# Modulation vectors as VectorE dot products along rows of turned weights, in a two-block transformer kernel on one core

## What is computed

```python
cond = silu(c)                                       # 1024 numbers
mod = (cond @ ada_w[l] + ada_b[l]).reshape(9, 1024)  # first block, nine vectors a layer
u = rmsnorm(h, gain) * (1.0 + mod[1]) + mod[0]
h = h + 0.5 * (1.0 + mod[2]) * swiglu(u, wg, wu, wd)
...
mod = silu(c_2) @ ada_w_2[l] + ada_b_2[l]            # second block, six vectors a layer
```

## Time and profile before

| | |
|---|---|
| runs | 2355.34, 2343.04, 2352.70 us; median 2352.7 |
| the profiled execution's own time | 2357.99 us |
| its span in the trace | 2356.2 us |
| mean granted TensorE clock | 0.961 of full speed |
| TensorE matmul busy | 2169.0 us (92%), 16352 matmuls |
| VectorE busy | 1649.2 us (70%) |
| ScalarE busy | 1055.9 us (45%) |
| GpSimd busy | 672.3 us (29%) |
| DMA | 465.39 MB, mean 198 GB/s |

### The profile page before, as it was taken

One profiled execution on the slowest core, in us unless ns is written; L12 is line 12 of the kernel. 1 busy time (PEld: TensorE's weight loads), 2 busy tenths in 40 slices (PEclk: granted clock), 3 DMA queues, 4 the chain that ended last, 5 costly groups with the idle time before them and its releaser, 6 DMA issues. The chain is left out here.

```text
span 2356.2 us, 38578 instructions
## 1 busy us (share of the span) xinstructions
PE 2169.0 (92%) x16352; PEld 2067.1 (88%) x16352; DVE 1649.2 (70%) x1821; ACT 1055.9 (45%) x1565; POOL 672.3 (29%) x294
## 2 busy tenths in 40 slices
PE   2999999989999998999899988999999888999998
PEld 2999898889999998888899976778999877879998
DVE  4777777787777777868767777865767867645555
ACT  2544566344445445563444354343444433435443
POOL 1233212212111121354233332423233424212222
PEclk9999999999999999999899988999999988998999
DMA  7677656457767776554477744545677643424553
GB/s 283 210 260 254 207 197 197 155 181 255 258 234 247 255 254 198 189 166 160 162 276 260 254 134 135 182 141 188 211 259 238 200 147 112 126 99 152 183 177 106
DMA packets 289789, 465.39 MB, mean 198 GB/s; under 512 B 11344, under 2 KB 231120, under 8 KB 289104
## 3 DMA queue, kind: packets, MB, share of 16 engines
q1 hardware_dynamic: 252320, 324.96, 42.4%
q10 hardware_dynamic: 37296, 137.97, 16.2%
HBM read 461.84 MB, written 1.05 MB: 196 GB/s over the span
## 5 line engine op out<-in xcount | busy, mean ns | idle before, releaser
L614 PE MATMUL bank<-u_high,high 128*128 128x256 f32 (+1 forms) x3248 | 943.1, 290 | 60.8 <-DVE u_low L1528 51.1
L614 PE MATMUL bank<-u_high,low 128*128 128x256 f32 (+1 forms) x3248 | 930.6, 287 | 0.0
L614 PE MATMUL bank<-u_low,high 128*128 128x256 f32 (+1 forms) x3248 | 930.5, 286 | 0.0
L1485 DVE TENSOR_TENSOR low<-ring,high 128x1024 fp32r<-128x1024 f32 x416 | 712.0, 1730 | 222.7 <-ACT high L1096 196.6
L1962 POOL TENSOR_TENSOR low<-ring,high 128x1024 fp32r<-128x1024 f32 x186 | 481.3, 2589 | 1258.4 <-ACT high L1096 1091.2
L614 PEld LDWEIGHTS bank<-u_high,high 128*128 128x128 f32 (+1 forms) x3248 | 628.8, 194 | 77.4 <-issue 48.4
L1096 ACT ACTIVATE high<-ring 128x1024 fp32r<-128x1024 f32 x602 | 601.1, 1042 | 160.7 <-PE bank L614 97.1
L614 PEld LDWEIGHTS bank<-u_low,high 128*128 128x128 f32 (+1 forms) x3248 | 624.8, 192 | 3.6 <-issue 2.7
L614 PEld LDWEIGHTS bank<-u_high,low 128*128 128x128 f32 (+1 forms) x3248 | 622.8, 192 | 0.4
L614 PE MATMUL bank<-xa,high 128*128 128x256 f32 x2368 | 433.7, 285 | 6.2 <-DVE low L1485 4.2
L614 PEld LDWEIGHTS bank<-xa,high 128*128 128x128 f32 x2368 | 370.6, 192 | 10.1 <-issue 4.9
(11 more groups left out here) (176 smaller groups left out, 2149.7 us busy)
## 6 DMA issues: line engine op xcount, KB each, us to landing
ada_ring<-ada ACTq DMA_DIRECT2D x256, 512.0 KB, 4.7
ring<-w_in SPq DMA_DIRECT2D x76, 1024.0 KB, 5.6
ring<-ffn_wg SPq DMA_DIRECT2D x44, 1024.0 KB, 6.4
ring<-ffn_wu SPq DMA_DIRECT2D x44, 1024.0 KB, 7.6
ring<-ffn_wd SPq DMA_DIRECT2D x44, 1024.0 KB, 5.9
ring<-ffn_w_gate_up SPq DMA_DIRECT2D x44, 1024.0 KB, 6.4
ring<-ffn_w_down SPq DMA_DIRECT2D x22, 1024.0 KB, 5.0
ring<-w_out SPq DMA_DIRECT2D x20, 1024.0 KB, 4.9
```

The source lines that it names most:

```text
L614: return pe.e.matmul(out, lhs, rhs, start=start, stop=stop, skip_group_check=True)
L1485: dve.e.tensor_tensor(lo, src, hi.bitcast(F32), ALU.subtract).then_inc(*dve.done(("low", n)))
```

## The change

A piece is now a slab of the turned weight: its 128 partitions are outputs, its free dimension the 1024 inputs. The host turns the weights (`layout`). Per piece VectorE makes one `scalar_tensor_tensor` that multiplies the slab with `cond`, which now lies in SBUF as a row of 1024 numbers per block copied to all 128 partitions, and sums along the row with `accum_out` into one column of `sums`. After a job's eight pieces VectorE adds the bias and writes `mods` in the same turn. ScalarE's `ada_high`, GpSimd's `ada_low`, the 16 matmuls of each job, their bank, and the tiles `ada_acc`, `ada_high`, `ada_low`, `ones_r` are gone. The loads of the pieces have the same sizes, queue, ring and waits as before. The two rows of `cond` (512 KB each) are two new loads on SyncE's queue, the first ahead of the parameters, the second behind the third fill; ScalarE applies Silu to 128 x 1024 for each, the second time between the issue of the constants and the first norm.

```diff
     def step(self):
-        total, self.split = self.split, self.full
-        split, self.full = self.full, None
...
-        return total, split, loads, piece
+        return loads, piece
...
     def until(self, job):
-        while JOB[job] not in self.summed:
+        while self.piece < KT * (JOB[job] + 1):
             yield self.step()
...
-        self.ada_acc = [self.sb(f"ada_acc{i}", D) for i in range(2)]
-        self.ada_low = [self.sb(f"ada_low{i}", D, F32R, at + 4 * D * i) for i in range(2)]
-        self.ada_high = self.sb("ada_high", D, F32R)
...
-        self.cond = self.sb("cond", 2 * KT)
+        self.cond = self.sb("cond", 2 * D)
+        self.sums = self.sb("sums", KT * len(JOBS))
...
-    def ada(turns):
-        for total, _, _, _ in turns:
-            if total is None:
-                continue
-            b = banks.take("work", "ada", total)
-            pe.wait_ge(("ada_low", total))
-            for j in range(KT):
-                mm(b[:, 2 * j:2 * j + 2], m.ada_high[:, j * P:(j + 1) * P], m.ones_r[:, 0:2], j == 0, False)
-                t = mm(b[:, 2 * j:2 * j + 2], m.ada_low[total % 2][:, j * P:(j + 1) * P], m.ones_r[:, 0:2], False, True)
-            t.then_inc(*pe.done(("ada_sum", total)))
...
     def ada(turns):
-        for _, split, loads, _ in turns:
-            if split is not None:
-                act.wait_ge(("ada", KT * split + KT - 1))
-                if split:
-                    act.wait_ge(("ada_sum", split - 1))
-                act.e.activation(m.ada_high[:, :], m.ada_acc[split % 2][:, :], ACT.Copy) \
-                    .then_inc(*act.done(("ada_high", split)))
+        for loads, _ in turns:
             for n in loads:
...
-    act.wait_ge(("params",), ("eps",), ("ones",))
-    act.e.activation(m.ones_r[:, :], m.ones[:, 0:2], ACT.Copy).then_inc(*act.done(("ones_r",)))
-    act.e.activation(m.cond[:, :], m.pc("c1", 0, 2 * KT), ACT.Silu).then_inc(*act.done(("cond",)))
+    act.wait_ge(("c", 0), ("eps",), ("ones",))
+    act.e.activation(m.cond[:, 0:D], m.cond[:, 0:D], ACT.Silu).then_inc(*act.done(("cond", 0)))
     ada(act.ada.until(("a", 1)))
...
     act.e.dma_start(m.cst[:, P:C1_W], dram["const1"][:, P:C1_W]).then_inc(*act.done(("c1",), sem="const", n=16))
+    act.wait_ge(("c", 1))
+    act.e.activation(m.cond[:, D:2 * D], m.cond[:, D:2 * D], ACT.Silu).then_inc(*act.done(("cond", 1)))
     for s in STAGES:
...
     def ada(turns):
-        for total, _, _, piece in turns:
...
-                dve.wait_ge(("cond",), ("ada_in", piece))
-                if k == 0:
-                    if job >= 2:
-                        dve.wait_ge(("ada_sum", job - 2))
-                    dve.e.tensor_scalar(to, w, m.cond[:, c:c + 1], None, ALU.mult).then_inc(*dve.done(("ada", piece)))
-                else:
-                    dve.wait_ge(("ada", piece - 1))
-                    dve.e.scalar_tensor_tensor(out=to, in0=w, scalar=m.cond[:, c:c + 1], in1=to, op0=ALU.mult,
-                                               op1=ALU.add).then_inc(*dve.done(("ada", piece)))
+        for _, piece in turns:
+            if piece is None:
+                continue
+            job, j = divmod(piece, KT)
+            block = "ab".index(JOBS[job][0])
+            w = m.ada_ring[:, piece % ADA_SLOTS * D:(piece % ADA_SLOTS + 1) * D]
+            dve.wait_ge(("cond", block), ("ada_in", piece))
+            dve.e.scalar_tensor_tensor(out=w, in0=w, scalar=1.0, in1=m.cond[:, block * D:(block + 1) * D],
+                                       op0=ALU.mult, op1=ALU.mult, accum_out=m.sums[:, piece:piece + 1]) \
+                .then_inc(*dve.done(("ada", piece)))
+            if j == KT - 1:
+                of = slice(KT * job, KT * (job + 1))
+                dve.wait_ge(("params",), ("ada", piece))
+                dve.e.tensor_tensor(m.mods[:, of], m.sums[:, of], m.pc("bias", KT * job, KT), ALU.add) \
+                    .then_inc(*dve.done(("mod", job)))
...
 def sp_program(sp, m, dram):
+    sp.e.dma_start(m.cond[:, 0:D], dram["cond"][:, 0:D]).then_inc(*sp.done(("c", 0), sem="c", n=16))
     sp.e.dma_start(m.par[:, :], dram["params"]).then_inc(*sp.done(("params",), sem="params", n=16))
...
         sp.e.dma_start(m.slot(n), f.source(dram)).then_inc(*sp.done(("fill", n), sem=f"fill{n % SLOTS}", n=16))
+        if n == 2:
+            sp.e.dma_start(m.cond[:, D:2 * D], dram["cond"][:, D:2 * D]).then_inc(*sp.done(("c", 1), sem="c", n=16))
...
-    ada1 = np.concatenate([i["ada_w"].reshape(LAYERS, D, 9, D).transpose(0, 2, 1, 3).reshape(LAYERS * 9, D, D),
+    ada1 = np.concatenate([i["ada_w"].reshape(LAYERS, D, 9, D).transpose(0, 2, 3, 1).reshape(LAYERS * 9, D, D),
...
+    cond = np.ascontiguousarray(np.broadcast_to(np.concatenate([i["c"][0], i["c_2"][0]])[None, :], (P, 2 * D)))
```

More of the change, by code:

```diff
@@ L59 @@
 PB_W = columns(PB, [("nm", 8), ("nf", 8), ("qn", 2), ("kvn", 1), ("gq", 1), ("gk", 1)])
-PC_W = columns(PC, [("c1", 8), ("c2", 8), ("fin", 8), ("out", 8), ("bias", 8 * len(JOBS))])
+PC_W = columns(PC, [("fin", 8), ("out", 8), ("bias", 8 * len(JOBS))])
 BASE_C = LAYERS * (PA_W + PB_W)
@@ L364, in __init__ @@
         self.piece = self.issued = 0
-        self.full = self.split = None
-        self.summed = set()
         self.due = 0.0
     def step(self):
-        total, self.split = self.split, self.full
-        split, self.full = self.full, None
-        if total is not None:
-            self.summed.add(total)
         loads = range(self.issued, min(self.piece + ADA_SLOTS, KT * len(JOBS)))
@@ L380, in step @@
             self.piece += 1
-            if piece % KT == KT - 1:
-                self.full = piece // KT
-        return total, split, loads, piece
+        return loads, piece
     def turns(self, rate):
@@ L706, in into_acc @@
             t.then_inc(*pe.done(("read", n)))
-            ada(pe.ada.turns(rate_of(keys[k])))
     def norm(s):
[L710 to L713, removed]
         b = banks.take("work", "norm", s)
@@ L996, in pe_program @@
         t.then_inc(*pe.done(("x_full", d // 2)))
-    pe.wait_ge(("ones_r",))
     for s in STAGES:
@@ L1005, in pe_program @@
             mixer2(s)
-        if s[0] not in ("fin", "out"):
-            ada(pe.ada.until(gate_of(s)[0]))
     for a in range(TT):
@@ L1941, in pool_program @@
 def pool_program(pool, m):
[L1942 to L1949, removed]
     def split(upto):
@@ L1968, in grains @@
             split(ahead_of(key))
-            ada(pool.ada.turns(rate_of(key)))
     def look_ahead(key):
@@ L1975, in norm @@
     def norm(s):
[L1976 to L1979, removed]
         look_ahead(first_grain(s))
@@ L2316, in parameters @@
         put(base, PB, "gk", column(np.tile(np.asarray(i["gqa_k_norm_g_2"][l]), 2), 1))
-    put(BASE_C, PC, "c1", column(i["c"][0], 8))
-    put(BASE_C, PC, "c2", column(i["c_2"][0], 8))
     put(BASE_C, PC, "fin", column(i["final_norm"], 8))
@@ L2345, in layout @@
     i = {k: np.asarray(v) for k, v in inputs.items()}
-    ada1 = np.concatenate([i["ada_w"].reshape(LAYERS, D, 9, D).transpose(0, 2, 1, 3).reshape(LAYERS * 9, D, D),
-                           i["final_ada_w"].reshape(D, 2, D).transpose(1, 0, 2)])
-    ada2 = np.ascontiguousarray(i["ada_w_2"].reshape(LAYERS, D, 6, D).transpose(0, 2, 1, 3)
+    ada1 = np.concatenate([i["ada_w"].reshape(LAYERS, D, 9, D).transpose(0, 2, 3, 1).reshape(LAYERS * 9, D, D),
+                           i["final_ada_w"].reshape(D, 2, D).transpose(1, 2, 0)])
+    ada2 = np.ascontiguousarray(i["ada_w_2"].reshape(LAYERS, D, 6, D).transpose(0, 2, 3, 1)
                                 .reshape(LAYERS * 6, D, D))
+    cond = np.ascontiguousarray(np.broadcast_to(np.concatenate([i["c"][0], i["c_2"][0]])[None, :], (P, 2 * D)))
     const1, const2 = constants()
     arrays = {n: np.ascontiguousarray(i[n]) for n in WEIGHTS}
-    arrays.update(x=np.ascontiguousarray(i["x"][0]), ada1=ada1, ada2=ada2, const1=const1, const2=const2,
+    arrays.update(x=np.ascontiguousarray(i["x"][0]), ada1=ada1, ada2=ada2, cond=cond, const1=const1, const2=const2,
                   params=parameters(i), na_bias=window_bias(i["na_rpb_2"]))
```

12 lines of the change are left out of this document (1 added, 11 removed).

## The result

The changed kernel takes 2288.9 us (median of 4 runs, 2286.1 to 2292.4) against 2352.9 for the kernel before, a ratio of 0.9744 with a 95% interval of 0.972 to 0.9767. The direction was right, the size was not. The profiled execution took 2291.4 us, 66.6 less than that of before. The changed kernel ran only with the result, so differences to it are good to some 3 us.

The account below looks back on a forecast made before the run. TensorE was taken to bound FFN stages, chains over other engines partly the mixers. Terms -33 - 7 - 4.5 + 2 + 5 = -37.5 us took the 2352.7 us median to 2315, range 2295 to 2339.

Parts of the forecast that it names:

- TensorE's matmuls: Removing each job's 16 matmuls saves 33 us in FFN stages, 7 in m1 and 4.5 in m2.
- GpSimd's subtractions: Removing GpSimd's 89.8 us over 30 jobs: an indirect gain through quicker VectorE, given no time in the sum.
- VectorE's pieces: Pieces with a row sum take 0.1 to 0.2 us more, hidden in FFN stages; net 2 us lost.
- the start: First fill 4 us earlier, but ScalarE waits for cond's second row before the first norm; 5 us lost.
- What bounds the kernel: FFN stages are TensorE's, by comparison with the last stage without jobs; mixers belong partly to chains over other engines.
- rival B: cond's second row lands early (9 us); mixers and slow FFN stage gain from GpSimd's relief (8 to 11); 2297; chance 0.20.
- FFN term: FFN stages: 19 jobs at 1.73 us of matmuls, all on the path, 33 us saved.
- The mixers' share: Matmuls removed in mixers: 70% of 10.4 us in m1 (7 us), half of 8.7 in m2 (4.5 us).
- ScalarE and GpSimd "counted at nothing": Neither engine is a bound; removing 31.4 us of ScalarE and 89.8 us of GpSimd gets no term in the sum.
- D: Row sum costs a second pass, 1.1 us more per piece; 76 us more, 2429 us; decisive from 0.6 us; chance 0.08.
- C: Only FFN stages gain; dearer pieces eat the mixers' share and the start loses 8 us; 2336 us; chance 0.12.
- E: Removal is worth nothing, TensorE's time for these matmuls being slack other engines fill; about 2350 us; chance 0.05.

Follow-up runs that it names:

- b_match: Kernel before with 64 bytes free before h and 32 before region, putting u and xa at the changed kernel's offsets within 128 bytes; 2334.9 us.
- a_mm: Changed kernel with 16 two-column matmuls per job put back on a tile of constants, without waits, result unread; 2315.4 us.
- a_pool: Changed kernel with one GpSimd subtraction of 128 x 768 on constants put back per job, 30 in all, result unused; 2303.7 us.
- a_back: Changed kernel with matmuls, GpSimd subtractions and the piece's scalar from SBUF put back together, without waits for other engines; 2328.9 us.
- a_twice: Changed kernel with each VectorE piece preceded by a second scalar_tensor_tensor on the same slab, without the sum, result unread; 2462.1 us.
- a_late: Changed kernel with cond's second row loaded behind fill 20 instead of 2, its Silu moved ahead of the first m1 stage's norm; 2277.9 us.
- b_up64: Kernel before with 64 bytes left free in front of h, putting u at 32 and xa at 64 within 128 bytes; 2330.0 us.
- a_up96: Changed kernel with 96 bytes left free in front of h, putting u at 0 and xa at 64 within 128 bytes; 2284.8 us.
- a_rel: As a_best, with the weight tiles high and low also moved by 64 bytes, so weights and moving operands all start at 64; 2284.6 us.
- a_best: Changed kernel with a_late's edit plus 32 bytes free before h and 64 before region, putting u and xa at 64; 2270.3 us.
- a_ptr: Changed kernel with the piece's constant scalar 1.0 read from a column of ones in SBUF; 2285.8 us, measured once.

## Why the prediction was wrong in size

| term | forecast, us | measured, us | by |
|---|---|---|---|
| places of `u` and `xa` | not in the sum | -15 | b_match |
| TensorE's matmuls | -44.5 | -26.5 | a_mm |
| GpSimd's subtractions | 0 | -15 | a_pool |
| VectorE's pieces, ScalarE, waits (6 to 8 us of it may be places) | +2 | -11 | left over, a_back |
| the start | +5 | +5 | first reciprocal |
| sum | -37.5 | -62.5 | -64 in all |

Without the 15 us of places the time would have been about 2304 us, inside the range; so the term that put the result below it is the one that the sum didn't have. That the rest comes near, -37.5 against -46, is in good part luck: the matmuls were put 18 us too high, GpSimd's subtractions 15 and the third group 13 too low.

**What bounds the kernel.** TensorE in the FFN stages was right, and reading it from the stage without jobs was the best step: its comparison gave 1.5 us per job for one stage and 2.9 for another, and a_mm gave 1.5. But the same comparison had 11.7 us for four jobs in the slow stage of the earlier trace rows, of which the matmuls are 6 to 7. I left the rest to rival B and held against it that the split of grains is unchanged; a_pool, in which that stage is 2.7 us longer than in the changed kernel, shows that GpSimd's subtractions are a part of it.

**TensorE's matmuls.** The mechanism held and the FFN term was near (28 for 33). The mixers' share was over-estimated: 11.5 us in the sum, about nothing in a_mm's total, with 5 us in the two m1 and no loss that shows in the two m2. There the failed step is taking a fixed share of TensorE's time in m2, where the trace shows chains over VectorE and ScalarE.

**ScalarE and GpSimd "counted at nothing".** Beside the places, this is the step of the argument that failed. Neither engine is a bound, and GpSimd idled 71% of the time, but of its 94 us of `ada_low` 76 overlapped VectorE's instructions on 128 x 1024, which take 1.3 us alone and up to 3.5 with it. I quoted the Trainium skill (SBUF — State Buffer, Who interferes with whom) for just this contention and then gave it a price only in rival B, together with an early landing that didn't come. The measured price is 15 us for 30 subtractions, 0.5 us each; the trace agrees with the rule.

**VectorE's pieces.** I expected 0.1 to 0.2 us more by ScalarE's accumulator row; the piece is 0.06 us shorter and its accumulator read adds 0.08 that overlaps the next instruction. Pieces in a row start 1.15 us apart, not 1.35. That FFN stages hide it was wrong for a dearer piece: a_twice shows 0.6 us lost per piece there at 1.2 us more, in stages where the changed kernel's VectorE is 77% busy. Idle time of an in-order engine that feeds the bound one is not slack to that amount. If the same holds in the other direction, a cheaper piece and quicker splits are worth something in FFN stages too.

**The start.** Right in mechanism and size: the second row was there at 55.3 us where 54 to 56 were forecast, the first u_high matmul was at 68.9 where 67.3 to 69.3 were, and the first reciprocal came 5.2 us later than before. SyncE's first fill was 2.7 us earlier, not 4. The loss is undone in a_late.

**The rivals.** D fell on its premise. The Trainium skill (Vector Engine (DVE) Microarchitecture Reference, Points that are easy to get wrong) says that this shape with two non-bf16 SBUF sources halves throughput for want of a port for the accumulator; the trace disagrees, 1.22 us for 1024 fp32 columns with the sum, 0.08 us for the accumulator. In a_twice the same instruction without the sum takes 1.22 us as well. Its price was under-estimated too: a_twice lost 173 us for 1.2 us per piece, so the point from which a dearer piece eats the whole gain lies near 0.3 us, not 0.6, if the loss grows in proportion, which no run here shows. C and E fell. B's 2297 is the nearest to the result, and its relief by GpSimd is shown; its other half, the early landing, is not what happened, and the places stand in no rival.

**What no step had.** That deleting tiles moves all tiles behind them: the sum went from one kernel's trace to the other as if the matmuls that stay kept their spacing. Nothing in the trace of before could give its price; the diff showed that 12 KB go in front of `h`, but only b_up64 and b_match say what that is worth, 22 and 15 us. The sum for equal places was -37.5 against -46, within the range's width.

## What to carry to other kernels

When an edit adds or removes a tile, every tile behind it moves; before crediting a gain of 1% to the edit (here 15 to 22 us of 2350), run the old kernel with its tiles padded to the new offsets. An engine that is 25% busy can still cost time by what it does to a neighbour's instructions: price its work by how long these get beside it, from the minimum and the maximum of their row. And what a new load's landing gates is found by listing what is queued behind the wait on the waiting engine; moving a wait past the work that covers it was worth 11 us here.

## What the runs showed of the hardware

- With weights and moving operand in SBUF at different distances within 128 bytes, back-to-back matmuls of 128 x 128 by 256 fp32r columns start 114.4 to 120.1 ns apart. Equal offsets gave 118.8 to 120.1 (before, a_up96, a_rel), a distance of 64 gave 114.4 (`xa` in a_up96), 115.8 (`xa` in a_best), 117.5 (`u` in a_best) and 118.0 (`xa` in b_up64), 32 gave 117.2 to 118.4, and 96 gave 120.0 and 120.1. That the same distance gives 114.4 and 118.0 shows that there is a second influence, which no run here isolates.
- A `scalar_tensor_tensor` with a sum along the row over 128 x 1024 fp32, both inputs in SBUF, takes 1.22 us, and a separate read of the accumulator 0.08 us. Without the sum it takes 1.22 us too (a_twice). A scalar from SBUF costs 0.06 us more than a constant (a_ptr).
- A VectorE instruction on 128 x 1024 fp32 with two inputs in SBUF takes 1.22 us in the median when it overlaps no GpSimd instruction and 2.56 us when it does (before; 2.53 in the changed kernel).
